# Decayed keys of the even mixer: made on VectorE instead of the Pool engine

## What is computed

```
f = lb + (1 - lb) * sigmoid(f_logit);  log_f = log(max(f, 1e-6));  key = 1 - f
per chunk:  cum = cumsum(log_f)
  scores[t,s] = sum_c q[t,c] * key[s,c] * exp(cum[t,c] - cum[s,c])   for s <= t
  out   = scores @ v + (q * exp(cum)) @ state
  state = exp(cum[last]) * state + (key * exp(cum[last] - cum))^T @ v
```

## Time and profile before

| | |
|---|---|
| median of 3 runs | 3540.65 us (3539.06 to 3543.72) |
| the profiled execution, its own time | 3540.75 us |
| span of its instructions | 3538.8 us |
| TensorE busy | 3470.5 us, 98% of the span |
| VectorE, Pool, ScalarE busy | 1643.1, 1797.5, 998.2 us |
| mean granted clock of TensorE | 0.995 |
| the four heads of the mixer | 1995 to about 2136 us of the span |

### The profile page before, as it was taken

How to read it: one execution, slowest core, us unless ns; L and a number is a source line. 1 busy time by engine, 2 the same in 40 slices (tenths; PEclk the granted TensorE clock), 3 DMA queues, 4 the chain that set the end, 5 groups by cost and what they waited for, 6 DMA issues and landing times.

```text
span 3538.8 us, 48832 instructions
## 1 busy us (share of the span) xinstructions
PE 3470.5 (98%) x18216; PEld 2774.4 (78%) x18216; DVE 1643.1 (46%) x2778; ACT 998.2 (28%) x1758; POOL 1797.5 (51%) x1056
## 2 busy tenths in 40 slices
PE   8999999999999999999999999999999999999999
PEld 6776778888877777888887787788887888788887
DVE  6466655435546574552531364345253135345342
ACT  4336532101233553220111233322012123332010
POOL 6432356656544334666565445356565522546655
PEclk9999999999999999999999999999999999999999
DMA  4220122323222112332332312133233233223322
GB/s 135 83 85 25 37 95 90 104 86 95 90 82 104 43 37 78 95 98 87 98 102 87 94 54 66 48 93 102 84 96 104 78 94 97 72 61 93 100 91 95
DMA packets 84945, 297.04 MB, mean 84 GB/s; under 512 B 9464, under 2 KB 11640, under 8 KB 84400
## 3 DMA queue, kind: packets, MB, share of 16 engines
q1 hardware_dynamic: 83296, 291.16, 26.2%
q0 software_dynamic: 1296, 3.15, 0.3%
q10 hardware_dynamic: 192, 0.47, 0.1%
HBM read 285.88 MB, written 8.86 MB: 83 GB/s over the span
## 4 chain that ended last, share of the span: by engine, by line
PE 90%; DVE 6%; ACT 2%; issue 1%; POOL 0%; DMA 0%; SPq 0%; ACTq 0%; DVEq 0%; POOLq 0%
PE PSUM L391 23%; PE PSUM L390 23%; PE PSUM L389 23%; PE PSUM L1087 2%; PE PSUM L1089 1%; PE PSUM L1088 1%; PE PSUM L2130 1%; DVE SLABS L1745 1%; DVE OUTER_PRODUCT L1742 1%; PE PSUM L2134 1%; PE PSUM L1127 1%; PE PSUM L1099 1%; PE PSUM L1111 1%; PE PSUM L1682 1%; PE PSUM L3119 0%
## 5 line engine op out<-in xcount | busy, mean ns | idle before, releaser
L300 POOL TENSOR_TENSOR W_LOS<-SLABS,W_HI 128x1024 fp32r<-128x1024 f32 (+3 forms) x454 | 1130.0, 2489 | 37.9
L298 POOL TENSOR_SCALAR W_HI<-SLABS 128x1024 fp32r<-128x1024 f32 (+3 forms) x454 | 499.6, 1100 | 1238.1 <-DMA SLABS<-w_k 1214.0
L390 PE MATMUL PSUM<-H_LO,W_HI 128*128 128x512 f32 x2448 | 966.9, 395 | 0.0
L389 PE MATMUL PSUM<-H_HI,W_HI 128*128 128x512 f32 x2192 | 870.0, 397 | 0.6 <-issue 0.6
L391 PE MATMUL PSUM<-H_HI,W_LOS 128*128 128x512 f32 x2192 | 870.5, 397 | 0.0
L390 PEld LDWEIGHTS PSUM<-H_LO,W_HI 128*128 128x128 f32 x2448 | 459.8, 188 | 117.1 <-issue 2.9
L389 PEld LDWEIGHTS PSUM<-H_HI,W_HI 128*128 128x128 f32 x2192 | 412.2, 188 | 100.2 <-issue 4.1
L391 PEld LDWEIGHTS PSUM<-H_HI,W_LOS 128*128 128x128 f32 x2192 | 411.5, 188 | 96.4
L558 DVE TENSOR_TENSOR PSUM<-PSUM,FACTORS 128x512 f32<-128x512 f32 x282 | 195.8, 696 | 564.7 <-PE PSUM L391 510.2
L389 PE MATMUL PSUM<-ACT_HI,W_HI 128*128 128x512 f32 x928 | 367.1, 396 | 1.7 <-DVE ACT_LO L519 1.7
L391 PE MATMUL PSUM<-ACT_HI,W_LOS 128*128 128x512 f32 x928 | 368.7, 397 | 0.0
(11 more groups left out here) (538 smaller groups left out, 4837.7 us busy)
## 6 DMA issues: line engine op xcount, KB each, us to landing
SLABS<-w_k SPq DMA_DIRECT2D x406, 512.0 KB, 3.5
SLABS<-w_k SPq DMA_DIRECT2D x32, 768.0 KB, 4.3
SLABS<-w_k SPq DMA_DIRECT2D x32, 640.0 KB, 3.9
X<-w_k SPq DMA_DIRECT2D x2, 2048.0 KB, 8.7
SLABS<-w_k SPq DMA_DIRECT2D x16, 256.0 KB, 2.9
ARENA<-gate_rows SPq DMA_DIRECT2D x8, 512.0 KB, 6.4
X<-xT SPq DMA_DIRECT2D x4, 512.0 KB, 6.4
gate_rows<-RT SPq DMA_DIRECT2D x8, 256.0 KB, 2.0
```

The source lines that it names most:

```text
L298: nc.gpsimd.tensor_scalar(hi, raw, 1.0, 0.0, MUL, ADD).then_inc(pool_step, 1)
L300: nc.gpsimd.tensor_tensor(lo, raw, hi.bitcast(F), SUB).then_inc(slab_split[s], 1)
L389: mm(out, w_hi, rhs[0](k), start=k == first, stop=False)
L390: mm(out, w_hi, rhs[1](k), start=False, stop=False)
```

## The change

`keys` moves from the Pool engine's list to VectorE's, right behind `queries` and ahead of `masked`, for 27 of its 28 instances. The first one (head 0, level 1) stays on the Pool engine, behind the clearing of the buffers. The counts of the semaphores are the same as before. In the Pool engine's list nothing stands any more between the other products.

```diff
+            def keys(h, lv):
+                b = LEVELS[lv - 1]
+                if (h, lv) == (0, 2):
+                    dve.wait_ge(mx["kl"], 1)
+                dve.wait_ge(mx["sc"], (NLV + 1) * h + lv - 1)
+                if lv == 2 and h:
+                    dve.wait_ge(*at("hk", h - 1))
+                nc.vector.tensor_tensor(lower_upper(KL[lv % 2], b)[0], lower_upper(HK[h % 2], b)[0], packed(EDEC[(lv - 1) % 2][:, 0:HALF], b),
+                                        MUL).then_inc(mx["kl"], 1)
+
             def masked(h, lv):
...
                 for lv in range(1, NLV + 1):
                     diff(h, lv + 1)
                     queries(h, lv)
+                    if h or lv > 1:
+                        keys(h, lv)
                     masked(h, lv - 1)
...
-            def keys(h, lv):
-                b = LEVELS[lv - 1]
-                pool.wait_ge(mx["e"], (NLV + 1) * h + lv)
-                used = (NLV + 1) * h + lv - 1
-                if used > 0:
-                    pool.wait_ge(mx["sc"], used)
-                if lv == 2 and h:
-                    pool.wait_ge(*at("hk", h - 1))
-                nc.gpsimd.tensor_tensor(lower_upper(KL[lv % 2], b)[0], lower_upper(HK[h % 2], b)[0], packed(EDEC[(lv - 1) % 2][:, 0:HALF], b),
+            def first_keys():
+                b = LEVELS[0]
+                pool.wait_ge(mx["e"], 1)
+                nc.gpsimd.tensor_tensor(lower_upper(KL[1], b)[0], lower_upper(HK[0], b)[0], packed(EDEC[0][:, 0:HALF], b),
                                         MUL).then_inc(mx["kl"], 1)
...
             for h in range(EV_HEADS):
                 for lv in range(1, NLV + 1):
-                    keys(h, lv)
+                    if (h, lv) == (0, 1):
+                        first_keys()
                     if lv == 2 and h == 0:
                         pool.wait_ge(even_in, need(even_in, 16))
                         ret_cos(0)
```

## The result

The changed kernel takes 3557.9 us in the median of 6 runs (3556.43 to 3562.09), against 3541.95 us for the kernel before on the same chip (6 runs). That is 16.0 us slower between the medians. The ratio, taken over all runs and not from the two medians, is 1.0048, 95% interval 1.0038 to 1.0059, so the loss is clear of noise. The forecast was 3557.5 us, 16.8 us more.

The account below looks back on a forecast made before the run. TensorE, busy 98% of the span, was taken to bound the kernel. To 3540.75 us the prediction added 11.7 us for the four heads and 5.1 us for the clock, 16.8 in all: 3557.5 us, range 3545 to 3565.

Parts of the forecast that it names:

- The bounds of the gain: TensorE's level products: removing every wait for the Pool's keys at no price would win 4.0 us, 0.11%.
- The price of one instance: Each keys product takes 0.33 us of VectorE's list, 8.9 us for 27; 0.42 us from start to end.
- the 2.1 us of the upper bound: Possible extra for writing every second element at levels 1 and 2: 7 x 0.3 us, at most 1.2 on the path.
- The added waits: Semaphore waits of the keys on VectorE cost nothing, as work ahead has already waited or the awaited product comes early.
- Turns: VectorE products of two SBUF inputs alternate with a row of Pool products: 1.41 us each in place of 0.33.
- Rival 2: VectorE isn't held by a row of Pool products; only 0.33 us per key on the path: 3543.3 us, 11%.
- The steps of head 2, without the clock: Level 2 +0.33 us, level 3 +2.77 with 2.4 idle, L2470 ending 6.2 after L2540's start, level 6 +4.08.
- The sum: Heads 0 to 3 without the clock: 1.2 + 4.1 + 4.1 + 2.3 = 11.7 us.
- Head 0: Queries and keys of level 3 each meet a ret_cos(0) product; level 4 starts 1.2 us later: +1.2 us.
- The clock: Five new TensorE idle times above 2 us; three followed by a low clock at 1.7 us each: +5.1 us.
- Rival 1: Turns happen but no further low clock: 3552.4 us, 27%.
- Rival 3: Not slower: all waits for keys go, if VectorE has over 0.33 us slack at levels 3 to 6: 3537.7 us, 9%.

Follow-up runs that it names:

- e1: Changed kernel with gated held until the keys of level 4 and ret_cos until those of level 6: 3541.45 us, ratio 1.0001.
- e4: Kernel before, all keys on the Pool engine, with gated moved up right behind ret_query: 3543.9 us, ratio 1.0007.
- e5c: Changed kernel plus products of constants in TensorE's idle times, in the cut-down counts (8, 4 and 1): 3550.38 us, ratio 1.0026.
- e9: Kernel before, queries of level 2 and exponential of level 6 made earlier, 4 products of constants in head 0, no holds: 3542.29 us, ratio 1.0004.
- e3: Changed kernel with only ret_cos held until the keys of level 6 are made: 3552.69 us, ratio 1.0029.

## Why the prediction was right

**The bounds of the gain.** Right. Of the waits for the Pool's keys (4.0 us) none is left, but 21.5 us for VectorE's stand in their place and in that of its queries.

**The price of one instance.** Right: 0.42 us, 0.33 to 0.34 to the next instruction, and 0.42 at levels 1 and 2 too. So in this case VectorE's write of every second element costs nothing extra, and the 2.1 us of the upper bound were not needed.

**The added waits.** No row shows a stop at them. The prediction argued this from the code, and it fits e1, in which they stand unchanged and the 16 us are gone.

**Turns.** Right in kind and size: from one start to the next it is 1.41 us, as put (2086.67, 2088.08, 2089.49), and from start to end 1.48. Rival 2 is out by the rows of head 2 and by e1 to e4.

**The steps of head 2, without the clock.** Level 2, +0.33 forecast: its idle time rose from 0.48 to 0.86. The trace names VectorE's keys as what it waits for; before it named nothing ("issue"), and that VectorE was the late one had been an inference. Level 3: forecast +2.77 since the head began; measured 91.12 - 77.71 = 13.41, less the 10.62 us that level 1 of this head was late already (2079.12 against 2068.50): +2.79. Idle time there: 2.4 forecast, 2.26 measured. L2470: 6.2 us after `ret_masked`, as forecast. Idle before level 6: the prediction gives no number, its sum makes it 0.84 + 4.08 - 2.77 = 2.15; measured 2.22.

**The sum.** Take each head from its level 1 to that of the next. With the clock kept at 1.00 (e5c), and 1.25 us taken off heads 0 and 3 of the kernel before for the one low stretch in each, the heads lengthened by 1.6, 4.3, 4.1 and 2.2 us. Forecast were 1.2, 4.1, 4.1 and 2.3: 11.7, measured 12.2.

**Head 0** came out by other steps than those written. The turns fell on L2495 and the queries of level 3, since VectorE had got less far in its list when the transfer let the Pool engine start (at 2004.34, with VectorE at L2494; before at 2002.49, with VectorE at L2495). The sum hardly differs, as the number of turns is the same. That the keys would meet the second product was wrong.

**The clock** is the part that was right for two wrong reasons. I put three added stretches at 1.7 us, 5.1. There were four more than before, at 1.25 us each (e5c), 5.0. That the two errors cancel is luck. The price of 1.7 is the work lost in the stretch; on the path it is less. Why I chose three of five had no row behind it. Rival 1 (no further low clock) is out by the six stretches in the trace. All five new idle times above 2 us were followed by one; it makes four, since the old one behind level 6 of head 3 is gone, where the idle time fell from 1.28 to 1.04 us.

**Rival 3**, not slower, had its condition wrong and not its sum: VectorE has most of the slack, as e1 shows (ratio 1.0001), but the Pool engine didn't keep clear. Even with `gated` and `ret_cos` held (e1), the gain of 3 us didn't come: TensorE's idle time in the mixer was 13.8 us against 12.5. The rule of the Trainium skill (GPSIMD Engine Reference, "Engine selection"), by which such products belong on VectorE, holds here for the instruction, 0.42 against 0.86 us in mean, but gained nothing for the kernel: after the reordering, keys on the Pool engine came out 2.6 us below keys on VectorE (0.9978 against 0.9987, whose intervals overlap). This doesn't show that the Pool engine is the better place. The two kernels differ in their holds too, and the one with keys on VectorE still waits for them 0.6 to 0.9 us at level 3.

## What to carry to other kernels

When an instruction leaves an engine's list, ask what stood behind it: here it had kept two rows of long Pool products apart from VectorE's critical ones, and two waits on a semaphore bring back all 16 us (1.3 us of it by the luck of the clock, as told at e1). Count a VectorE product of two SBUF inputs beside a row of Pool products as one turn each, and place the Pool's work in VectorE's pauses on purpose, not by where other work happens to end. An idle time on TensorE costs its length and, when a low clock follows, about a microsecond more (1.25 us by the traces, 1.0 by the medians).

## What the runs showed of the hardware that I had not expected

Engines wait for each other through semaphores, as the start of this document says, but not through them alone: no semaphore stands behind these waits. The turns are strict wherever a row of Pool products met VectorE in the mixer of these traces: after a Pool product of 128x512 one VectorE instruction goes, then the next Pool product, with VectorE's 0.41 us growing to 1.48 and the Pool's 1.27 to 1.45. An operation with one full-size input in SBUF is held in the same way: L2472, 0.54 us alone, took 1.43 beside `ret_cos` in e9. The operations that read PSUM keep their time beside a Pool product: in e9 L2550 starts inside one at 2083.97 and takes 0.69 us, as it does alone.

Which idle time is followed by a low clock was not settled, and its length alone doesn't say. The 1.28 us of head 3 in the kernel before was; 1.28 at the same place in e4 and 1.04 in e1 weren't. In e3 a stretch began at level 2 of head 0, behind 1.14 us, which in the changed kernel (1.15) and in e1 was not followed by one. And the 2.38 us of head 1 in e3 and the 1.82 and 1.71 us before level 6 in e9 were followed by none, while 2.38 us at the same place of the changed kernel were.
